# Modulation sums moved from VectorE to GpSimd, and the gather ticks and head choices of a fused transformer kernel placed anew

## The chip, the cores and the metric

The kernel runs on one core of a Trainium2 chip. The metric is the device time of one execution in microseconds, as the median of several runs. Before the change it is 1738.4 us (three runs, 1738.04 to 1740.64).

## What is computed

The input is one sequence of 256 rows by 1024 columns, in float32 throughout. A first block applies four mixers in turn (gated linear attention, a gated spatial unit, forgetting attention, gated linear attention again), each wrapped in an adaptive norm. A second block has a hybrid of convolution and dilated attention, and then a PEER layer: for every row, 8 heads choose 16 experts each out of 128 x 128, and every chosen expert is one row of a "down" table and one of an "up" table.

```python
def first_block(...):
    cond = silu(c)
    for i in range(DEPTH):                       # 4 mixers
        mod = (cond @ w_mod[i] + b_mod[i])[:, None, :]
        shift, scale, gate = split(mod, 3)
        h = rms_norm(x, norm_pre_g[i]) * (1.0 + scale) + shift
        ...                                      # mixer i on h, times gate, added to x
def peer_ffn(u, w_query, sub_keys, expert_down, expert_up):
    s = einsum('thcd,hckd->thck', q, sub_keys)
    top_s, top_i = top_k(s, 16)
    cand_s = top_s[:, :, 0, :, None] + top_s[:, :, 1, None, :]
    best_s, pos = top_k(cand_s.reshape(...), 16)
    idx, gates = take_along_axis(cand_i, pos), softmax(best_s)
    a = gelu(einsum('cd,ced->ce', u, expert_down[idx]))
    return einsum('ce,ced->cd', gates * a, expert_up[idx])
```

## The kernel before, in words

The 256 rows are two tiles of 128 partitions. One list, `ORDER` (made by `make_order`, line 357), holds every step of both tiles, and each engine walks the same list and emits its own share of each step; semaphores join the shares. A step `mm` (`project`, line 948) multiplies one block of 512 columns of a weight: 8 products of 128x128 by 128x512, whose weights SyncE loads into a ring of four halves of 1 MB. The first tile runs through all its mixers while blocks of the second tile are put into its gaps; behind that come the second tile's remaining blocks, and last its PEER layer alone.

**Modulation.** `cond @ w_mod` is a sum over eight slices k of the weight for each layer L and each third (shift, scale, gate): 96 pieces of 128x1024. A piece is fetched, and VectorE adds piece times cond's column into a sum (`add_piece`, line 1567). The first 16 come through `early` tiles, loaded by SyncE; six of these (`PE_PIECES`) are multiplied on TensorE instead (`piece_columns`, line 986). The other 80 are fetched by GpSimd's queue into a ring of four (`fetch`, line 849), each fetch behind a wait until VectorE has used the ring's place. The sums' biases are set by `start_sums` (lines 856 and 857), the gains behind the mixers are fetched by `fetch_post` (line 863). `mod_cols` (lines 1010 and 1831) turns shift and scale of a layer into columns, `mod_gate` (lines 1019 and 1839) spreads the gate over the partitions. `pieces_at` says behind which block the pieces are added: ahead of that block's own evacuation.

**Levels.** A gated linear attention mixer has seven levels (`level`, line 964). For each, VectorE makes exponents with two products of two operands in SBUF (lines 1581 and 1582), ScalarE takes their exponential (line 1365), VectorE multiplies twice more (lines 1590 and 1592), TensorE multiplies, and VectorE merges (line 1601).

**PEER.** `choose` (lines 1732 to 1781) finds one head's 16 experts in four parts. A `tick` is one chosen expert of all 128 rows: GpSimd issues its gathers (line 877), VectorE takes the product of the down row with the input (line 1798), ScalarE takes gelu of a group of these (line 1486, groups in `GROUPS`), VectorE forms the coefficients (line 1790), and `LEAD` ticks later the up row is added, on VectorE (line 1813) or on TensorE (lines 1493 and 1203). In the first tile, down and up rows are two gathers of 0.5 MB for each of 128 ticks; in the second, one gather of 1 MB. `Rows` hands out the ticks among the second tile's blocks by way gone (`WAY`), at most three behind a block (`spot`). Parts of the next head's choice hang on ticks 2, 4, 6 and 8 of a head.

## Time and profile before

| what | value |
|---|---|
| median of 3 runs | 1738.4 us |
| the profiled execution's own time | 1739.41 us |
| its span, first to last instruction | 1737.6 us |
| busy PE, DVE, ACT, POOL | 1393.7, 1047.5, 433.1, 490.7 us |
| mean granted TensorE clock | 0.909 |
| read from HBM | 589.55 MB, 340 GB/s over the span |

PE is TensorE, PEld its weight loads, DVE VectorE, ACT ScalarE, POOL GpSimd, SP SyncE; a q behind a name is its queue. In a row of the timeline the first number is the start and the second the length, both in us; what stands in brackets at its end is how long the engine was idle before it and what ended the idleness. The L numbers are lines of the kernel.

### The profile page before, as it was taken

How to read it: one execution, taken by the hardware profiler on the slowest of the kernel's cores; microseconds unless marked ns; L12 is line 12 of the kernel's file. 1: busy time of each engine (PE TensorE's matmuls, PEld its weight loads, DVE VectorE, ACT ScalarE, POOL GpSimd, SP SyncE). 2: the span in 40 equal slices, each digit the busy share in tenths (PEclk: the TensorE clock that was granted, in tenths of full speed). 3: DMA queues.
4: the chain of work that ended last, by engine and by line, in shares of the span. 5: the costliest groups of instructions: out<-in, count | busy, mean ns of one | idle time of the engine just before them, and what ended most of it. 6: DMA issues, size and time to landing. Idle time of an engine off the chain costs nothing. (4 is left out here: it accounts for less than half of the span.)

```text
span 1737.6 us, 13867 instructions
## 1 busy us (share of the span) xinstructions
PE 1393.7 (80%) x4158; PEld 717.6 (41%) x4158; DVE 1047.5 (60%) x2197; ACT 433.1 (25%) x974; POOL 490.7 (28%) x498
## 2 busy tenths in 40 slices
PE   6998988978999999999777777699787647666665
PEld 6454435444444455444354343455333312222222
DVE  3645554553233222313797998788866778877876
ACT  1221413423423421102133232132002221111111
POOL 2101210210000000000445546355344545444441
PEclk9998998989999999999897888798888878898898
DMA  9978884978556776887999989999999999999995
GB/s 386 377 256 303 312 340 171 347 282 295 213 207 219 277 265 242 290 293 265 402 361 357 413 339 403 412 400 413 410 414 414 348 412 422 421 422 421 422 421 248
DMA packets 108941, 591.53 MB, mean 340 GB/s; under 512 B 12450, under 2 KB 12706, under 8 KB 60612
## 3 DMA queue, kind: packets, MB, share of 16 engines
q0 software_dynamic: 67776, 312.56, 45.4%
q1 hardware_dynamic: 41092, 278.10, 42.2%
q8 instruction: 34, 0.56, 0.1%
q14 instruction: 39, 0.32, 0.0%
HBM read 589.55 MB, written 1.05 MB: 340 GB/s over the span
## 5 line engine op out<-in xcount | busy, mean ns | idle before, releaser
L948 PE MATMUL bank<-ring,hT 128*128 128x512 f32 x1888 | 866.6, 615 | 39.6 <-DVE room L1920 12.1
L948 PEld LDWEIGHTS bank<-ring,hT 128*128 128x128 f32 x1888 | 366.5, 198 | 482.2 <-issue 449.8
L877 POOL DMA_INDIRECT room<-in_peer_down,idx x92 | 102.5, 1114 | 525.1 <-DVE idx L1781 401.8
L1798 DVE CUSTOM_DVE_ANT_0 room<-room 128x1024 f32<-128x1024 f32 x180 | 218.6, 1221 | 50.6 <-DMA room<-in_pair,idx 38.4
L1203 PE MATMUL bank<-room 128*128 128x512 f32 x284 | 150.9, 676 | 96.5 <-ACT room L1493 94.2
L1813 DVE SCALAR_TENSOR_TENSOR x<-room,pcoef,x 128x1024 f32<-128x1024 f32 x121 | 155.7, 1287 | 28.0 <-DMA room<-in_peer_up,idx 27.5
L877 POOL DMA_INDIRECT room<-in_peer_up,idx x104 | 114.0, 1096 | 88.6 <-DVE pa L1798 42.3
L1203 PEld LDWEIGHTS bank<-room 128*128 128x128 f32 x284 | 57.5, 215 | 190.8 <-issue 97.2
L849 POOL DMA_DIRECT2D room<-in_w_mod x80 | 42.2, 528 | 326.3 <-DVE room L1567 206.5
L877 POOL DMA_INDIRECT room<-in_pair,idx x88 | 97.0, 1102 | 108.5 <-PE bank L1203 50.6
L927 PE MATMUL bank<-cst,room 128*128 128x128 f32 x424 | 64.7, 297 | 55.3 <-ACT room L1439 24.1
L1203 PE MATMUL bank<-ring,room 128*128 128x512 f32 x116 | 72.6, 774 | 38.0 <-ACT room L1493 38.0
L1567 DVE SCALAR_TENSOR_TENSOR room<-room,cst 128x1024 f32<-128x1024 f32 x58 | 74.4, 1282 | 36.0 <-DMA room<-in_w_mod 26.8
L927 PEld LDWEIGHTS bank<-cst,room 128*128 128x128 f32 x424 | 54.9, 153 | 82.4 <-ACT room L1439 26.8
L964 PE MATMUL bank<-room 128*128 128x128 f32 x256 | 43.9, 331 | 34.7 <-DVE room L1592 34.7
L1493 ACT ACTIVATE room<-cst,pcoef 128x128 f32<-128x128 f32 x102 | 36.8, 392 | 118.0 <-DVE pcoef L1790 110.8
L1439 ACT ACTIVATE room<-room,anm 128x128 f32<-128x128 f32 (+1 forms) x80 | 35.4, 443 | 116.3 <-DVE anm L2004 116.3
L877 POOL DMA_INDIRECT ring<-in_pair,idx x40 | 46.6, 1166 | 61.8 <-PE bank L1203 30.8
L1798 DVE CUSTOM_DVE_ANT_0 ring<-ring,room 128x1024 f32<-128x1024 f32 x40 | 48.8, 1226 | 23.1 <-DMA ring<-in_pair,idx 22.8
L1203 PEld LDWEIGHTS bank<-ring,room 128*128 128x128 f32 x116 | 26.7, 243 | 80.6 <-ACT room L1493 52.3
L964 PEld LDWEIGHTS bank<-room 128*128 128x128 f32 x256 | 40.0, 236 | 44.9 <-DVE room L1592 40.1
L1272 ACT ACTIVATE room<-bank 128x512 f32<-128x512 f32 x24 | 14.3, 596 | 147.0 <-PE bank L948 147.0
(304 smaller groups left out, 1527.4 us busy)
## 6 DMA issues: line engine op xcount, KB each, us to landing
ring<-in_wpk SPq DMA_DIRECT2D x248, 1024.0 KB, 7.0
room<-in_w_mod POOLq DMA_DIRECT2D x80, 512.0 KB, 8.2
room<-in_w_mod SPq DMA_DIRECT2D x8, 1024.0 KB, 15.8
room<-in_norm_post_g POOLq DMA_DIRECT2D x4, 512.0 KB, 5.0
rowb<-in_gate_bias SPq DMA_DIRECT2D x4, 512.0 KB, 9.0
room<-in_peer_up,idx POOLq DMA_INDIRECT x104, 12.5
room<-in_peer_down,idx POOLq DMA_INDIRECT x92, 12.4
room<-in_pair,idx POOLq DMA_INDIRECT x88, 14.3
```

What stands on the lines that cost most here:

```text
L849: pool.dma_start(mring[n % 4], w[:, k, third * D:(third + 1) * D]).then_inc(S(f"pool_in{n % 4}"), 16)
L877: return pool.indirect_dma_start(out=dst, out_offset=None, in_=A[table][0] if table != "pair" else A[table], in_offset=bass.IndirectOffset ...
L927: last = tr(cols4(b, i), src(i), ident)
L948: last = mm(bank[p][:, :], lhs, ring[:, h % 4, k * N:(k + 1) * N], start=(kk == 0), stop=(h == halves[-1] and k == 3))
L964: last = mm(cols4((b, c, a)[l % 3], h), k_[:, h * P:(h + 1) * P], q_[:, h * P:(h + 1) * P], start=True, stop=True)
L1203: last = mm(bank[WORK[tile][i]][:, :], diag[:, nth % 4, :], row[:, i * N:(i + 1) * N], start=(v == mine[0]), stop=(v == mine[-1]), skip_gr ...
L1272: af(dst, src, ACT.Copy).then_inc(done, 1)
L1439: last = af(s, s, ACT.Exp, bias=anm[:, t, n, h:h + 1], accum_out=al[:, t, n, h:h + 1])
L1493: af(diag[:, nth % 4, :], ident, ACT.Copy, scale=pcoef[:, v // TOPK % 4, v % TOPK:v % TOPK + 1]).then_inc(S("diag"), 1)
L1567: v.scalar_tensor_tensor(out=a, in0=piece, scalar=const("cond", k, 1), in1=a, op0=ALU.mult, op1=ALU.add).then_inc(S("summed"), 1)
L1798: v.tensor_tensor_reduce(out=row, in0=row, in1=u_(g // MINE), scale=1.0, scalar=0.0, op0=ALU.mult, op1=ALU.add, accum_out=pa[:, g // TOPK ...
L1813: v.scalar_tensor_tensor(out=x[:, tile, :], in0=row, scalar=pcoef[:, w, e:e + 1], in1=x[:, tile, :], op0=ALU.mult, op1=ALU.add) \
```

## The change

1. Pieces: the first 16 go to VectorE but for two on TensorE (six before). Of the 80 others, the 24 scales of layers 1 to 3 stay on VectorE and the 56 shifts and gates go to GpSimd, as two instructions each (a product, then a sum), through a ring of two places; the scales have the other two. `mod_cols` and `mod_gate` wait for GpSimd's count. VectorE's pieces now stand behind a block's own work. GpSimd's queue also carries the fetches of scales, some behind a wait for VectorE.
2. Ticks: also between the second tile's levels. The last eight picks are added two a tick, the last group of four is two of two, and four ticks at the end fall away. In `make_order` one block of the second tile stands earlier.
3. Choices: the first head's score is transposed and multiplied one block sooner, and its choice stands a block sooner. In the first tile a head's parts stand in the list by themselves, behind blocks with little VectorE work, or when they are due. Inside `choose`, casts fall away, and pairs of instructions over both halves become one.

```diff
-            "gap twice"]
+            "gap" if L == 2 else "gap twice"]
...
             b(3, [], [("unit", t, 1), ("forget_sum", t)]),
+            "gap",
...
-            b(0, name="query", pre=[("norm_in", t, 5)]),
-            b(1, [("score_T", t, 0)], name="query"),
-            b(2, [("score_S", t, 0), ("score_T", t, 1)], name="query"),
+            b(0, [] if t else [("score_T", t, 0)], name="query", pre=[("norm_in", t, 5)]),
+            b(1, [("score_T", t, 0)] if t else [("score_S", t, 0)], name="query"),
+            b(2, ([("score_S", t, 0)] if t else []) + [("score_T", t, 1)], name="query"),
...
-TICKS = PICKS + REST + LEAD[1]
-PE_PIECES = (5, 7, 9, 11, 13, 15)
+TICKS = PICKS + REST + 2
+FIRST = [(0, third, k) for third in range(2) for k in range(KC)]
+PE_PIECES = (5, 7)
+DVE_FIRST = len(FIRST) - len(PE_PIECES)
+DVE_PIECES = [(L, 1, k) for L in range(1, DEPTH) for k in range(KC)]
+POOL_PIECES = [(0, 2, k) for k in range(KC)] \
+    + [(L, third, k) for L in range(1, DEPTH) for third in (0, 2) for k in range(KC)]
...
 def added_at(v):
+    if v >= PICKS - 8:
+        return tick_of(PICKS - 2) + (v - PICKS + 8) // 2
     return tick_of(v) + LEAD[v // MINE]
...
+    def choose_light(self, most):
+        for _ in range(most):
+            if self.part < 4 * PH and self.at >= TOPK * (self.part // 4 - 1) - 6:
+                self.choose_next()
+    def choose_due(self):
+        while self.part < 4 * PH and self.at >= TOPK * (self.part // 4 - 1) + 3 + 2 * (self.part % 4):
+            self.choose_next()
...
+            elif s[0] == "level" and after[0] in ("level", "cross"):
+                spot(1)
...
+            def fetch(i):
+                if i >= len(POOL_PIECES):
+                    return
+                if i >= 2:
+                    pool.wait_ge(S("pool_summed"), i - 1)
+                pool.dma_start(mring[i % 2], piece_of(*POOL_PIECES[i])).then_inc(S(f"pool_in{i % 2}"), 16)
+            def fetch_scale(i):
+                pool.wait_ge(S("summed"), DVE_FIRST + max(i - 1, 0))
+                pool.dma_start(mring[2 + i % 2], piece_of(*DVE_PIECES[i])).then_inc(S(f"pool_in{2 + i % 2}"), 16)
+            def add_piece(i):
+                L, third, k = POOL_PIECES[i]
+                pool.wait_ge(S(f"sums_init{L % 2}"), sums_set(L))
+                pool.wait_ge(S(f"pool_in{i % 2}"), (i // 2 + 1) * 16)
+                link(nc.gpsimd.tensor_tensor(mring[i % 2], mring[i % 2], const("cond", k, 1).to_broadcast([P, D]), ALU.mult))
+                if i:
+                    pool.wait_ge(S("pool_summed"), i)
+                nc.gpsimd.tensor_tensor(sums[L % 2][third], sums[L % 2][third], mring[i % 2], ALU.add) \
+                    .then_inc(S("pool_summed"), 1)
+                fetch(i + 2)
...
+            pool.wait_ge(S("summed"), DVE_FIRST)
+            for i in range(2):
+                fetch(i)
+            for i in range(2):
+                fetch_scale(i)
+            for k in range(KC):
+                add_piece(k)
+                if k % 2:
+                    fetch_scale(2 + k // 2)
...
-                    pe.wait_ge(S("summed"), summed_before((L + 1) * 3 * KC))
+                    pe.wait_ge(S("pool_summed"), gates_of(L))
```

## Rows read from the trace of the kernel before

**Rows 1.** The page's slices: 40 equal parts of the span, and bytes moved.

```profile
PE   6998988978999999999777777699787647666665
...
GB/s 386 377 256 303 312 340 171 347 282 295 213 207 219 277 265 242 290 293 265 402 361 357 413 339 403 412 400 413 410 414 414 348 412 422 421 422 421 422 421 248
```

**Rows 2.** Stretches: length, busy PE, PEld, DVE, ACT, POOL, clock, DMA share, GB/s.

```profile
60.00:440.00 380.00, 328.99 (x1033) 175.02 (x1032) 193.18 (x334) 114.97 (x246) 48.30 (x87) 0.92 0.79 295
440.00:820.00 380.00, 363.07 (x1121) 182.55 (x1119) 105.64 (x286) 96.15 (x209) 0.00 (x0) 0.99 0.71 253
820.00:1380.00 560.00, 433.19 (x1420) 237.60 (x1420) 447.70 (x922) 140.29 (x309) 273.00 (x246) 0.87 0.98 391
```

**Rows 3.** The same view, stretches of 20 us.

```profile
900.00:920.00 20.00, 12.38 (x72) 11.17 (x70) 16.81 (x31) 9.18 (x17) 9.34 (x9) 0.68 0.80 278
1020.00:1040.00 20.00, 13.94 (x43) 8.79 (x44) 18.32 (x53) 9.77 (x23) 6.52 (x6) 0.83 0.75 269
1080.00:1100.00 20.00, 20.00 (x64) 10.02 (x63) 12.86 (x32) 3.46 (x5) 7.99 (x8) 1.00 1.02 415
```

**Rows 4.** Groups of instructions by line and form: busy us, mean ns, idle before.

```profile
L1567 DVE SCALAR_TENSOR_TENSOR room<-room,cst 128x1024 f32<-128x1024 f32 x58 | 74.4, 1282 | 36.0 <-DMA room<-in_w_mod 26.8 <-DMA room<-in_b_mod 8.0
L856 POOL MEMSET room<- 128x1024 f32 x8 | 7.8, 970 | 0.0
L1581 DVE TENSOR_TENSOR room<-room 128x256 f32<-128x256 f32 x28 | 11.7, 417 | 0.6 <-DVE room L1892 0.5
```

**Rows 5.** DMA issues, median us from issue to landing.

```profile
room<-in_w_mod POOLq DMA_DIRECT2D x80, 512.0 KB, 8.2
```

**Rows 6.** The timeline from 20 to 60 us: the first layer's columns.

```profile
25.49 13.65 PE L986 MATMUL bank<-cst,room 128*128 128x1 f32 x64
29.20 1.28 DVE L1567 SCALAR_TENSOR_TENSOR room<-room,cst 128x1024 f32<-128x1024 f32 x1 [1.27 <-DMA room<-in_w_mod]
46.00 0.17 DVE L1831 COPY modc<-bank 128x8 f32<-128x8 f32 x1 [15.52 <-PE bank L1010]
```

**Rows 7.** The timeline: a decay, and where the sums of layers 0 to 2 are due.

```profile
68.27 0.69 DVE L1615 SCALAR_TENSOR_TENSOR room<-bank,room 128x512 f32<-128x512 f32 x1 [2.44 <-ACT room L1354]
...
98.03 1.02 PE L1019 MATMUL bank<-room,ones 128*128 128x512 f32 x2
...
148.15 2.25 PE L1010 MATMUL bank<-ones,room 128*128 128x1 f32 x16
...
154.53 0.16 DVE L1831 COPY modc<-bank 128x8 f32<-128x8 f32 x1
...
287.54 3.63 PE L1010 MATMUL bank<-ones,room 128*128 128x1 f32 x32
```

**Rows 8.** TensorE's waits from 60 to 440 us: total, times, longest.

```profile
PE bank L964 <- DVE room L1592: 13.6, 7, 3.1
PE bank L948 <- DVE room L1920: 8.4, 3, 5.0
PE bank L1123 <- DVE room L1986: 7.1, 2, 4.4
PE bank L1019 <- DVE gateb L1839: 5.7, 1, 5.7
```

**Rows 9.** The timeline around the first head's choice.

```profile
811.26 0.49 DVE L1732 MAX8 pv<-room 128x8 f32<-128x128 f32 x2 [10.83 <-ACT room L1474]
821.25 1.00 POOL L877 DMA_INDIRECT room<-in_peer_down,idx  x1 [393.95 <-DVE idx L1781]
```

**Rows 10.** The timeline behind the second tile's last levels.

```profile
1023.05 1.24 POOL L877 DMA_INDIRECT room<-in_peer_up,idx  x1 [6.88 <-DVE pa L1798]
```

**Rows 11.** The timeline of the last 15 us.

```profile
1722.75 1.22 DVE L1798 CUSTOM_DVE_ANT_0 room<-room 128x1024 f32<-128x1024 f32 x1 [1.21 <-DMA room<-in_pair,idx]
1724.57 5.42 PE L1203 MATMUL bank<-room 128*128 128x512 f32 x12 [1.20 <-ACT room L1493]
1730.02 1.28 DVE L2086 TENSOR_TENSOR x<-x,bank 128x512 f32<-128x512 f32 x2 [0.72 <-PE bank L1203]
```

More of the change, by code:

```diff
@@ L272 @@
 DVE_NTH = {u: i for i, u in enumerate(ON_DVE)}
-ADDS = {added_at(v): [v] for v in range(PICKS)}
+ADDS = {k: [v for v in range(PICKS) if added_at(v) == k] for k in range(TICKS)}
 def adds_of(k):
-    return ADDS.get(k, [])
+    return ADDS[k]
 def sums_at(hh):
@@ L302, with light @@
        "z_T": 15, "att_in": 20, "b_T": 20, "merged_T": 40, "ffn_norm": 60, "score_T": 6, "score_S": 10}
+DVE_WORK = {"norm_in": 5, "low": 2, "decay": 25, "qk_T": 4, "level": 20, "cross": 25, "heads": 25, "post0": 7,
+            "post1": 50, "center": 30, "mix": 35, "unit": 40, "forget": 5, "forget_sum": 5, "quad_S": 27, "quad_V": 6,
+            "fox_gate": 14, "rotary": 18, "merge": 50, "z_T": 65, "b_T": 14, "ffn_norm": 20}
+def light(steps):
+    return sum(DVE_WORK.get(s[0], 0) for s in steps) <= 12
 def way_of(step):
@@ L320, in __init__ @@
         self.order, self.at, self.added = order, 0, 0
+        self.part = 4
     def add_next(self):
@@ L367, in make_order @@
             second.append(c)
-    done, pending, ahead, piece = 0, [], False, 2 * KC
+    done, pending, ahead, piece = 0, [], False, 0
     for c in first:
@@ L379, in make_order @@
             order.append(mm)
-        for _ in range(pieces_at(mm)):
-            if piece < len(PIECES):
-                order.append(("mod", piece))
-                piece += 1
         if mm and mm[2] in ("out0", "out1", "out2") and mm[3] == 1:
@@ L397, in make_order @@
                 order.append(("sines", 0))
+            for _ in range(PIECES_AT[name][n] if name in PIECES_AT else 0):
+                order.append(("mod", piece))
+                piece += 1
             order += pending
             pending = []
-            if name == "query" and n == 2:
-                order.append(("choose", 0))
-                rows.tick()
-            if name == "query" and n == 3:
-                rows.tick()
-                rows.tick()
+            if name == "query" and n == 1:
+                order += [("choose", 0, part) for part in range(4)]
+            if name == "query" and n >= 2:
+                for _ in range(n - 1):
+                    rows.tick()
     order += pending
@@ L432, in make_order @@
             if s == ("score_S", 1, 0):
-                order.append(("choose", PH))
+                order += [("choose", PH, part) for part in range(4)]
             if (s[0], after[0]) in (("quad_S", "quad_P"), ("cross", "heads")):
                 spot(2)
+            elif s[0] == "level" and after[0] in ("level", "cross"):
+                spot(1)
         if not (i + 1 < len(left) and left[i + 1][0]):
             spot(3)
+        if light(post):
+            rows.choose_light(2)
+    assert rows.part == 4 * PH
     while rows.at < TICKS:
@@ L992, in _ @@
             pe.wait_ge(S("cond"), 1)
-            for piece in PE_PIECES[:2]:
+            for piece in PE_PIECES:
                 piece_columns(piece, use("mod_cols", 0)[1])
@@ L2076, in _ @@
                 elif kind == "choose":
-                    for part in range(4):
-                        choose(t, part)
+                    choose(t, step[2])
                 elif kind == "tick":
```

146 lines of the change are left out of this document (74 added, 72 removed).

## The prediction

> **What bounds the kernel now.** I read the page's slices first. They show three stages: up to about 820 us TensorE is nearly always busy and the bytes stay far under their best rate; from there to 1380 us the rate is mostly over 400 GB/s and TensorE falls back; behind that it is 412 to 422 [rows 1]. The stretches put numbers to it: from 60 to 440 us TensorE is busy 329 of 380 us at a clock of 0.92, from 440 to 820 us 363 of 380 at 0.99, from 820 to 1380 us the DMA share is 0.98 [rows 2]. So up to 820 us the time is TensorE's with what it waits for, and behind that it is mostly the gathers'. An earlier start of the gathers moves the end with it, one for one, as long as nothing else becomes late.
>
> What is open before 440 us: 51 us of TensorE idleness, and 0.08 of the clock, 380 x 0.08 = 30 us. The waits name VectorE for most of it: 13.6 us at the levels, 8.4 behind the mixer's output, 7.1 before the scores, and one of 5.7 before a gate [rows 8]. What is open from 820 to 1380 us: at 391 GB/s on average against 415 in a full stretch, 560 x (1 - 391/415) = 32 us of transfer time [rows 2, 3]. Two of the holes are at 900 and 1020 us, of 20 x (1 - 278/415) = 6.6 and 20 x (1 - 269/415) = 7.0 us [rows 3].
>
> **The change, part by part.** The sum is made against the profiled execution's own 1739.4 us; the median of the runs shown is 1.0 lower.
>
> *The first columns.* TensorE spent 13.65 us on four pieces (64 records), to 39.1 us, and then made the columns, so that they were copied at 46.0; VectorE's last of ten pieces stood at 29.2 [rows 6]. With four more pieces of 1.28 [rows 4] among its 10, VectorE ends at about 33.4, and the columns, which took 46.0 - 39.1 = 6.9 us, need half of that behind it, as the shifts' half can go ahead: 37. That is 9 us sooner.
>
> *GpSimd's chain up to layer 1.* It takes what was won back. GpSimd has no arithmetic with operands in the trace of before; the nearest row is its memset of the same shape, 0.97 us, which only writes [rows 4]. From below I bound one instruction by that, from above by three times it, 2.9 (two reads and a write, one behind another). VectorE's 1.28 with two operands lies between. I take 2.4, toward the upper end, because nothing in the row says that reads are free. A piece is then 2 x 2.4 + 0.3 = 5.1 us. Each ring place goes round in 5.1 + 0.3 + 8.2 (issue to landing, [rows 5]) = 13.6 us, and there are two places: 6.8 us a piece. The first fetch waits for VectorE's 14 pieces (33.4) and lands near 44. The third piece stands behind a fetch of a scale that waits until VectorE has added its first one, behind the decay, whose first step stood at 68.3 [rows 7] and whose end now comes at some 62: 4.5 us more. The gates of layer 0, 8 pieces, then stand at about 99, where they were used at 98.0 and would now be wanted at 89 [rows 7]. Layer 1's shifts, 16 pieces: 44 + 7 x 13.6 + 6.3 + 5.1 + 4.5 = 155, and columns and copy 4.4 later, 159.5. Before, the copy was at 154.5 [rows 7]. So the term is **+5**, with the first columns' 9 us inside it. With 0.97 an instruction the chain is not late, and what is left is 9 sooner and 4 because VectorE no longer adds pieces right ahead of the copy: -13. With 2.9 it is +14. Layer 2's columns are due at 287.5 [rows 7] and need 32 pieces, which stand at 155 + 16 x 6.8 = 264; layer 3's are due later still for as many more. That cover is gone at over 8.2 us a piece. No gather waits in GpSimd's queue, for the first is at 821 [rows 9].
>
> The Trainium skill (GPSIMD Engine Reference, Elementwise) gives 4497 ns for such an addition of 2048 elements a partition, by which I would estimate 2.25 us for 1024; by it this term would be about +3. No run here shows it yet.
>
> *VectorE's relief, 60 to 440 us.* Of 90 pieces on VectorE 38 stay; 52 x 1.28 = 67 us go [rows 4]. Most of this lay beside TensorE. What TensorE waited for behind pieces I bound by the longest wait of each row, 3.1 + 5.0 + 4.4 + 5.7 = 18.2, and half of the 16.6 that these rows have besides: 26 us [rows 8]; the clock would give part of its 30 besides. I take half of the 26, **-12** rounded, and nothing for the clock, since other waits remain and will be late next (ScalarE's exponentials between a level's halves, the sums of squares). Ends: -40 (all 26 and half the clock) and 0.
>
> *The stage of gathers.* The first choice began at 811.3, when the score had come, and the first gather went out at 821.3 [rows 9]; one block sooner is about 8 us, in which VectorE still has to end the second tile's `unit` work. At 270 GB/s instead of 415 there, 8 x (1 - 270/415) = 2.8: **-3**. Ticks between levels and choices moved behind lighter blocks: GpSimd stood 6.9 us behind VectorE at the end of the levels [rows 10]; of the 14 us in the two holes I take half, **-7**. The casts saved in `choose` are under 1 us a head and lie beside transfers: 0. The ticks between levels make the second tile's levels longer, which costs nothing while transfers bind. Ends of this part: 0 and -25.
>
> *The end.* The last row's product starts at 1722.75; then come gelu, coefficients, three adds on TensorE (5.42 us from 1724.57), and the final sum at 1730.02 [rows 11]. Afterwards only picks 254 and 255 are left then, both on VectorE, two adds of 1.28 [rows 4] from about 1725.3: 1727.9. **-2**, ends -3 and 0.
>
> Sum: 1739.4 + 5 - 12 - 3 - 7 - 2 = 1720.4; less the 1.0 to the median, 1719.5. A measurement of this kernel tells about 0.2%, 3.5 us, from no change.
>
> **The rivals.**
>
> *A: GpSimd and VectorE stop each other (slower).* While a GpSimd instruction reads SBUF, VectorE's instructions with two operands in SBUF wait for its end. The place is the levels of layer 0 in both tiles, 14 levels with two pairs of such products each of 0.42 us [rows 4], with GpSimd busy 4.8 of 6.8 us. One wait of about 2.4 us a pair is 28 x 2.4 = 67 us on VectorE; half uncovered makes +34, and the other work up to 440 us +10. Instead of -19 the sum is +25: 1763. It decides from about 1.0 us a pair (28 x 1.0 / 2 = 14, and 4 for the rest), where the gain of 19 is gone. For it: TensorE already waited 13.6 us at the levels [rows 8], so there is no slack there. Against it: nothing in the trace of before shows VectorE slowed by GpSimd, though GpSimd reads no tensor there. Chance 0.23. This is a rule of the Trainium skill too (SBUF — State Buffer, Who interferes with whom): the second of the two to issue blocks fully until the first is done. No run here shows it yet.
>
> *B: the gain stays small (no change).* The chain is +5, VectorE's relief is a third (-4), because TensorE's own work is what is left, and of the gathers' part only -1: about 1739. For it: the clock below 1.0 stays whatever is idle. Chance 0.10.
>
> *C: only the gathers' side pays.* The relief is eaten by a later chain (+10, -12), and -8 comes behind 820 us, the end with it: 1728. Chance 0.15.
>
> *D: all open parts close.* -13 - 26 - 17 - 3 = -59: 1680. For it: the row of memset. Chance 0.07.
>
> *E: the ticks' new places do nothing*, since DMA is full anyway at 0.98 [rows 2]: 1727, taken together with C.
>
> **How the numbers follow.** The forecast has 0.45, for 1719.5. The range goes from 1700, half way to D, to 1758, most of the way to A; outside are D and the upper half of A. Faster: 0.45 + 0.15 + 0.07 = 0.67; no change 0.10; slower 0.23.
>
> **What would show it.** The `modc` copy of layer 1 at about 159 us; GpSimd's products and sums at 2 to 2.9 us; VectorE's lines 1581 to 1592 still at 0.42 us (rival A shows them longer, or TensorE's wait at the levels at 30 us and more); TensorE's stretch from 60 to 440 us some 12 us shorter to the same step; the first gather before 808; the holes behind the levels half filled; 5 us from the last landing to the final sum. Wrong would be: a gate's or column's wait of over 10 us for GpSimd, or a first gather later than 821.

## The result, and the profile after it

The changed kernel takes 1805.84 us (median of 4 runs, 1801.42 to 1810.19), the kernel before on the same chip 1739.52 (4 runs). The ratio is 1.0377, with a 95% interval from 1.0346 to 1.0409: slower by 66 us, where 19 us faster was forecast. The profiled execution has a span of 1799.6 us, against 1737.6 before; it is the shortest of the four runs, so the tables below account for 62 us and not for 66.

Three moments split both spans: the first gather, the first gather of a pair (where the second tile's own work is done), and the last row's product.

| | before | after | difference | forecast |
|---|---|---|---|---|
| to the first gather (stage A) | 821.3 | 860.0 | +38.7 | -10 |
| to the first gather of a pair (stage B) | 573.6 | 596.9 | +23.3 | -7 |
| to the last row's product (stage C) | 327.9 | 329.6 | +1.7 | 0 |
| to the end | 14.8 | 13.2 | -1.6 | -2 |

The forecast column puts each term into the stage in which it begins. Of a choice made 8 us sooner the prediction counted only 3 us for the end, so it had the first gather itself before 808, and gave some of that back in stage B.

The page of the kernel after: its slices, its groups of GpSimd's products and sums and of VectorE's scale pieces, and the landing of the pieces.

```profile
PE   5767876998798999999885856869987746666765
...
GB/s 387 307 227 287 279 316 230 213 331 247 238 205 184 262 254 262 257 318 249 389 411 314 359 373 326 366 355 413 415 415 415 371 387 420 421 420 421 421 420 264
...
L908 POOL TENSOR_TENSOR room<-room,cst 128x1024 f32<-128x1024 f32 x56 | 108.1, 1930 | 15.6 <-DMA room<-in_w_mod 12.3
...
L911 POOL TENSOR_TENSOR room<-room 128x1024 f32<-128x1024 f32 x24 | 60.4, 2515 | 1.9
...
L902 POOL DMA_DIRECT2D room<-in_w_mod x24 | 12.8, 533 | 107.1 <-DVE room L1652 107.1
L1652 DVE SCALAR_TENSOR_TENSOR room<-room,cst 128x1024 f32<-128x1024 f32 x24 | 46.6, 1940 | 15.6 <-DMA room<-in_w_mod 15.2
...
room<-in_w_mod POOLq DMA_DIRECT2D x80, 512.0 KB, 5.3
```

GpSimd's instructions came as estimated (1.93 and 2.5 us for the 2.4 assumed), and the pieces land sooner than in [rows 5] (5.3 us, not 8.2). So the lengths of GpSimd's own instructions are not what was mis-sized. But the same VectorE sum that took 1.28 us in [rows 4] takes 1.94 here, and L902 shows 107.1 us in which GpSimd stood, with its own pieces behind it, at fetches that wait for VectorE.

Stretches, with the columns of [rows 2]:

```profile
60.00:440.00 380.00, 299.80 (x916) 160.73 (x915) 220.56 (x266) 98.22 (x212) 253.47 (x175) 0.87 0.73 265
...
860.00:1457.00 597.00, 454.69 (x1466) 247.95 (x1464) 452.41 (x881) 146.37 (x322) 296.68 (x257) 0.87 0.96 378
```

In the same 380 us TensorE does 916 matmuls where it did 1033, at a clock of 0.87 for 0.92. VectorE, which should have been relieved, is busy 221 us where it was 193. TensorE's waits in that stretch, beside [rows 8] (L1044 and L1100 are L964 and L1019 of before):

```profile
PE bank L1044 <- DVE room L1677: 39.7, 9, 6.1
PE bank L1100 <- DVE gateb L1915: 11.4, 1, 11.4
PE bank L1028 <- DVE room L1996: 9.8, 3, 6.8
```

The timeline, 76.66 to 89.07 us, in the first tile's levels of layer 0:

```profile
77.33 0.41 DVE L1667 TENSOR_TENSOR room<-room 128x256 f32<-128x256 f32 x1
77.77 0.43 DVE L1675 TENSOR_TENSOR room<-room 128x256 f32<-128x256 f32 x1
78.10 2.17 POOL L908 TENSOR_TENSOR room<-room,cst 128x1024 f32<-128x1024 f32 x1 [0.25 <-DMA room<-in_w_mod]
78.11 0.42 DVE L1677 TENSOR_TENSOR room<-room 128x256 f32<-128x256 f32 x1
78.56 2.00 DVE L1666 TENSOR_TENSOR room<-room 128x256 f32<-128x256 f32 x1
...
80.36 2.40 POOL L911 TENSOR_TENSOR room<-room 128x1024 f32<-128x1024 f32 x1
80.48 2.55 DVE L1667 TENSOR_TENSOR room<-room 128x256 f32<-128x256 f32 x1
82.96 0.41 DVE L1675 TENSOR_TENSOR room<-room 128x256 f32<-128x256 f32 x1
...
83.30 2.55 DVE L1677 TENSOR_TENSOR room<-room 128x256 f32<-128x256 f32 x1
...
85.63 2.43 POOL L911 TENSOR_TENSOR room<-room 128x1024 f32<-128x1024 f32 x1
85.76 0.72 DVE L1686 COPY_PREDICATED room<-gmask,bank 128x512 f32<-128x512 int32 x1
85.90 1.78 PEld L1044 LDWEIGHTS bank<-room 128*128 128x128 f32 x8 [5.69 <-DVE room L1677]
```

A level product takes 0.41 us while GpSimd computes nothing (77.33, 82.96), and 2.00 or 2.55 us when a product or sum of GpSimd is under way: it ends when GpSimd's ends (78.56 + 2.00 = 80.56; 80.48 + 2.55 = 83.03). The one at 78.11 starts together with GpSimd's product and keeps its 0.42 us; there the product is the longer one, 2.17 us for a mean of 1.93. TensorE then waits 5.7 us where [rows 8] had 3.1 at most. This is rival A as it was written, and the rule of the Trainium skill (SBUF — State Buffer, Who interferes with whom), that the second to issue blocks fully; the trace agrees.

### The profile page after: what moved, and what is told of

It is laid out like the page before. It is cut to its first block and busy times, and to the rows that moved or that the text cites. A ratio compares the mean times of both kernels' runs of the same rounds, so it can differ in the third digit from the quotient of the medians.

```text
span 1799.6 us, 13758 instructions
## 1 busy us (share of the span) xinstructions
PE 1397.9 (78%) x4094; PEld 713.6 (40%) x4094; DVE 1079.9 (60%) x2050; ACT 436.0 (24%) x977; POOL 759.7 (42%) x610
## 5 line engine op out<-in xcount | busy, mean ns | idle before, releaser
L1874 DVE CUSTOM_DVE_ANT_0 room<-room 128x1024 f32<-128x1024 f32 x174 | 211.4, 1221 | 62.8 <-DMA room<-in_pair,idx 41.1
L1284 PE MATMUL bank<-room 128*128 128x512 f32 x284 | 160.1, 713 | 95.5 <-ACT room L1575 93.3
L1889 DVE SCALAR_TENSOR_TENSOR x<-room,pcoef,x 128x1024 f32<-128x1024 f32 x127 | 163.4, 1286 | 36.1 <-DMA room<-in_peer_up,idx 35.4
L957 POOL DMA_INDIRECT room<-in_peer_up,idx x110 | 129.0, 1172 | 84.6 <-DVE pa L1874 34.1
L1284 PEld LDWEIGHTS bank<-room 128*128 128x128 f32 x284 | 61.1, 227 | 193.0 <-issue 103.5
L1007 PE MATMUL bank<-cst,room 128*128 128x128 f32 x424 | 66.1, 300 | 68.2 <-DVE room L1618 27.3
L908 POOL TENSOR_TENSOR room<-room,cst 128x1024 f32<-128x1024 f32 x56 | 108.1, 1930 | 15.6 <-DMA room<-in_w_mod 12.3
L1044 PE MATMUL bank<-room 128*128 128x128 f32 x256 | 49.0, 355 | 75.1 <-DVE room L1677 75.1
L1284 PE MATMUL bank<-ring,room 128*128 128x512 f32 x116 | 65.5, 705 | 39.2 <-ACT room L1575 39.2
L1044 PEld LDWEIGHTS bank<-room 128*128 128x128 f32 x256 | 44.0, 256 | 86.3 <-DVE room L1677 81.6
L911 POOL TENSOR_TENSOR room<-room 128x1024 f32<-128x1024 f32 x24 | 60.4, 2515 | 1.9
L902 POOL DMA_DIRECT2D room<-in_w_mod x24 | 12.8, 533 | 107.1 <-DVE room L1652 107.1
L1652 DVE SCALAR_TENSOR_TENSOR room<-room,cst 128x1024 f32<-128x1024 f32 x24 | 46.6, 1940 | 15.6 <-DMA room<-in_w_mod 15.2
(305 smaller groups left out, 1720.4 us busy)
```

The lines of the kernel that those rows point to most:

```text
L908: link(nc.gpsimd.tensor_tensor(mring[i % 2], mring[i % 2], const("cond", k, 1).to_broadcast([P, D]), ALU.mult))
L911: nc.gpsimd.tensor_tensor(sums[L % 2][third], sums[L % 2][third], mring[i % 2], ALU.add) \
L957: return pool.indirect_dma_start(out=dst, out_offset=None, in_=A[table][0] if table != "pair" else A[table], in_offset=bass.IndirectOffset ...
L1007: last = tr(cols4(b, i), src(i), ident)
L1044: last = mm(cols4((b, c, a)[l % 3], h), k_[:, h * P:(h + 1) * P], q_[:, h * P:(h + 1) * P], start=True, stop=True)
L1284: last = mm(bank[WORK[tile][i]][:, :], diag[:, nth % 4, :], row[:, i * N:(i + 1) * N], start=(v == mine[0]), stop=(v == mine[-1]), skip_gr ...
```

## Experiments

Ratios are to runs of the kernel before on the same chip. "A" is the first gather, "B" the stage behind it, both from one profiled execution. One kernel was profiled twice and gave 808.6 and 812.2 for A, and the kernels whose stage B is as before or nearly so give 572.7 to 578.0 for B (in one case 582.2); smaller differences than these say nothing by themselves. "The lock" is short for what the last timeline shows: an instruction of VectorE and one of GpSimd of which one waits for the other's end.

### The parts of the change

**Modulation alone** (pieces to GpSimd, VectorE's scale pieces, the first columns; nothing of ticks, choices, gaps or end):

```
(in words) POOL_PIECES, DVE_PIECES, add_scale, fetch_scale and PIECES_AT as in the change;
           make_order's ticks, choices and gaps, and the end, as in before
```

> The kernel before with the modulation part of the change alone (shifts and gates on GpSimd, pieces' new places, two pieces on TensorE). Theory 1 (GpSimd and VectorE stop each other, and that is most of the loss): first gather some 35 to 50 us later than before's 821 us, in all 1775 to 1790 us; the level products (128x256, two operands in SBUF) near 0.9 us again instead of 0.42. Theory 2 (the loss comes from the new places of ticks and choices): within 5 us of before. The changed kernel's stage of gathers was 23 us longer too; if that is the ticks' doing, this run shows none of it: from first gather to first gather of the second tile 574 us as before.

1775.71 us, 1.0151 (1.0111 to 1.0190); A 852.7, B 577.5. By the ratio this part costs 26 us (19 to 33), by the first gather 31; B is within what unchanged kernels show.

**Everything but the modulation:**

```
(in words) all hunks of the change but those of sums, pieces and PIECES_AT;
           pieces_at, add_piece and PE_PIECES as in before
```

> The changed kernel with the modulation as before: only ticks, choices, the tail and the blocks' order are changed. Theory 1 alone: faster than before by some 5 to 12 us. If the new places of ticks and choices are a loss by themselves, as the 23 us longer stage of gathers in the changed kernel suggests: 1750 to 1765 us, with the first gather some 8 us sooner than before's 821 us and the stage of gathers near 597 instead of 574 us.

1759.94 us, 1.0086 (1.0056 to 1.0116); A 817.1, B 596.4. Slower too: 4 us sooner in A, which is within what one kernel shows, and 23 lost in B. So there are two losses, and each shows without the other: the two spans are 38.1 and 20.1 us longer than before's, 58 together, where the whole change has 62. In A they do not simply add up: the modulation part is worth 31 us alone (852.7 for 821.3) and 43 beside the rest (860.0 for 817.1). Why is open.

**The first columns alone:**

```
-PE_PIECES = (5, 7, 9, 11, 13, 15)
+PE_PIECES = (5, 7)
```

> The kernel before with pieces 9, 11, 13 and 15 on VectorE instead of TensorE, nothing else. The first layer's columns are copied near 37 instead of 46 us. If nothing later holds, 1730 us (9 less); if VectorE's pieces from 48 us on hold the end of the first mixer anyway, 1736 to 1739 us.

1741.85 us, 0.9981 (0.9960 to 1.0001), not told from no change. The columns are copied at 36.92 instead of 46.0 (37 forecast), yet A is 821.5 (821.3 before). What is won is lost again later: layer 1's columns come at 151.0 for 154.5, layer 3's at 445.6 in both. One row also made it look larger than it is: in the traces of kernels with the old first columns the copy stands anywhere from 42.2 to 46.2, so the columns come 5 to 9 us sooner.

### The lock

**Memsets for GpSimd's product and sum** in the kernel after (the kernel leaves shifts and gates out of the result):

```
-nc.gpsimd.tensor_tensor(mring[i % 2], mring[i % 2], cond, ALU.mult)
+2 x nc.gpsimd.memset(mring[i % 2], 0.0)
-nc.gpsimd.tensor_tensor(sums, sums, mring[i % 2], ALU.add)
+3 x nc.gpsimd.memset(sums, 0.0)
```

> The changed kernel, with GpSimd's product replaced by two memsets and its sum by three of the same tile (4.9 us a piece against 4.4): the same waits and places, the modulation's shifts and gates left out. Theory 1a (VectorE waits because GpSimd reads SBUF): level products back at 0.42 us and TensorE's wait at the levels near 14 us; first gather 825 us or sooner, in all 1755 to 1770 us. Theory 1b (the loss is the length of GpSimd's chain, not the lock): first gather still at 855 to 870 us, in all 1800 us or more.

1784.69 us, 1.0217 (1.0178 to 1.0257); A 842.5, B 596.0. Groups of VectorE with their forms up to the first gather, this kernel, and below it the kernel after:

```profile
L1654 DVE SCALAR_TENSOR_TENSOR room<-room,cst 128x1024 f32<-128x1024 f32 x24 | 30.8, 1282 | 55.7 <-DMA room<-in_w_mod 55.4
...
L1668 DVE TENSOR_TENSOR room<-room 128x256 f32<-128x256 f32 x21 | 8.8, 418 | 0.6 <-DVE room L1970 0.5
```

```profile
L1666 DVE TENSOR_TENSOR room<-room 128x256 f32<-128x256 f32 x21 | 24.2, 1154 | 0.6 <-DVE room L1968 0.5
...
L1686 DVE COPY_PREDICATED room<-gmask,bank 128x512 f32<-128x512 int32 x24 | 17.3, 722 | 6.8 <-PE bank L1044 6.4
```

Without GpSimd's reads every VectorE form with two operands in SBUF is back at its old duration; the one that copies out of a PSUM bank (L1686, 0.72 us) was never longer. So the lock is shown, and it is worth 17 us of A (860.0 to 842.5); if anything that is too little, for memsets hold up other forms of VectorE (last section). But theory 1a had 825 or sooner, and 842.5 is still 25 us behind the 817.1 of the kernel with the old modulation: a second cause.

**The lock with nothing moved**, and its comparison. The kernel before, with work for GpSimd on the free ring place ahead of each fetch:

```
 def fetch(n):
     pool.wait_ge(S("summed"), ...)
+    2 x nc.gpsimd.tensor_tensor(mring[n % 4], mring[n % 4], cond, ALU.mult)   (first run)
+    4 x nc.gpsimd.memset(mring[n % 4], 0.0)                                  (second run)
```

> The kernel before, nothing moved, with two products of GpSimd (128 partitions by 1024, both operands in SBUF) on a free place of the ring ahead of each of its 80 fetches of a piece; VectorE still adds all 90 pieces. If GpSimd's reads stop VectorE (theory A), VectorE's sums of 1.28 us and its level products of 0.42 us come out at 1.6 to 2.5 us wherever GpSimd is at it, and the kernel takes 15 to 40 us more than the same kernel with memsets in their place. If the lock needs something else of the change, both kernels take the same time to 4 us.

> The kernel before with four memsets of GpSimd (about 0.97 us each, nothing read) ahead of each fetch of a piece, as the comparison for the run with two products: the fetches are held up about as long. Theory A: VectorE's sums stay at 1.28 us and its level products at 0.42 us; the time is that of the kernel before or up to 8 us more, for the later fetches alone.

1874.55 us, 1.0772 (1.0733 to 1.0811), against 1813.74 us, 1.0406 (1.0365 to 1.0446). One row of each, groups of VectorE with their forms from 60 to 500 us, first the products, then the memsets:

```profile
L1569 DVE SCALAR_TENSOR_TENSOR room<-room,cst 128x1024 f32<-128x1024 f32 x41 | 103.7, 2529 | 26.6 <-DMA room<-in_w_mod 25.8
```

```profile
L1569 DVE SCALAR_TENSOR_TENSOR room<-room,cst 128x1024 f32<-128x1024 f32 x44 | 56.4, 1283 | 68.4 <-DMA room<-in_w_mod 67.9
```

1874.55 - 1813.74 = 61 us is the lock, above the 15 to 40 expected: 160 products of 2.1 us, and VectorE's sum of 1.28 takes 2.53. The comparison missed its own bound of 8 us by far (it lost 72): the pieces' fetches come late by four memsets each, and VectorE waits 105 us for them (67.9, 27.3 and 10.1 in its three groups). The ring of pieces was no place with slack.

### The rest of stage A

In the run with memsets VectorE stood 35 us at its first scale piece of layer 2; in the modulation part alone 17.6 us, and there GpSimd stood 21.6 us at the fetch of the next one. The timelines of the two kernels, first VectorE with memsets, then VectorE and GpSimd of the modulation alone:

```profile
210.17 1.29 DVE L1654 SCALAR_TENSOR_TENSOR room<-room,cst 128x1024 f32<-128x1024 f32 x1 [34.96 <-DMA room<-in_w_mod]
```

```profile
205.82 1.28 DVE L1620 SCALAR_TENSOR_TENSOR room<-room,cst 128x1024 f32<-128x1024 f32 x1 [17.56 <-DMA room<-in_w_mod]
...
233.20 2.65 DVE L1620 SCALAR_TENSOR_TENSOR room<-room,cst 128x1024 f32<-128x1024 f32 x2
234.78 0.54 POOL L870 DMA_DIRECT2D room<-in_w_mod  x1 [21.55 <-DVE room L1620]
```

Both engines work in order, and each has work behind a wait for the other: VectorE the second tile's levels behind a piece that GpSimd has not fetched, GpSimd its own pieces behind a fetch whose place VectorE has not read.

**VectorE's pieces of layer 2 later**, in the kernel with memsets and in the modulation part alone:

```
-"in1": (1, 2, 2, 2, 1, 0)
+"in1": (0, 0, 2, 2, 2, 2)
```

> The kernel after with GpSimd's product and sum replaced by memsets of the same cells (shifts and gates are left out of the result), and VectorE's eight scale pieces of layer 2 put one to two blocks later in its order. Theory I (VectorE works in order, and a scale piece for which GpSimd has not even issued the fetch holds the second tile's levels behind it, 35 us in the run with memsets): the wait of 35 us is gone or under 10, and the first gather comes at 815 to 825 us instead of 842.5, the kernel at 1755 to 1767 instead of 1784.7. Theory F (GpSimd's fetches are simply too late for layer 2, wherever VectorE asks for them): the columns of layer 2 are as late as in the run with memsets (323 us) and the first gather stays past 835 us.

> The modulation part alone (1775.7 us), with VectorE's eight scale pieces of layer 2 one to two blocks later in its order. Theory I (VectorE's scale pieces and GpSimd's fetches of them stand in two queues that wait for each other): TensorE's wait of 17.0 us at the second tile's levels of layer 1 goes, the first gather comes 10 to 15 us sooner than 852.7, and the time is 1761 to 1767 us. Theory G (the lock and GpSimd's pace are all there is): the first gather stays within 4 us of 852.7 and the time over 1771 us.

With memsets: 1771.44 us, 1.0157 (1.0128 to 1.0185), A 828.6, between the two theories; 14 of the 25 us come back. With the lock: 1777.79 us, 1.0219 (1.0181 to 1.0256), A 851.8: nothing. Theory I failed there. The wait only moved: TensorE now stands 22.5 us at the second tile's levels, at 273.8, because VectorE's pieces come one for each piece of GpSimd, 6.6 us apart (fetched at 238.5, 245.2, 251.9, 258.5).

**The fetches by SP:**

```
(in words)
-GpSimd: fetch_scale(i) between its own pieces
+SP, ahead of the weights two blocks on: wait for the sum of piece i - 2, then fetch piece i
```

> The modulation part alone (1775.7 us), with the 24 fetches of VectorE's scale pieces issued by SP, two blocks ahead of their use, instead of by GpSimd between its own pieces. Theory K (VectorE's scale pieces come at GpSimd's pace, one for each product and sum of GpSimd, 6.6 us apart, and GpSimd itself stands up to 21.6 and 31.6 us behind VectorE at such fetches; both waits come from the shared queue): these waits go, TensorE's waits of 17.0 and 11.1 us at 213 and 266 us are under 8 together, the first gather comes at 835 to 845 us instead of 852.7, the time is 1758 to 1768. Theory G (the lock alone is what costs): the first gather stays over 849 us.

> The same fetches by SP in the kernel in which GpSimd's product and sum are memsets (1784.7 us; shifts and gates are left out of the result), with the ticks between levels and the choices' places of the change. With neither the lock nor the shared queue left, theory K gives the first gather at 812 to 822 us, as with the modulation part of before (817.1), or sooner by what the prediction hoped for (12 us); the stage of gathers stays at 596 us and the time comes to 1752 to 1764. If the first gather stays past 830 us, GpSimd's pace of 5.8 us a piece is a cause of its own.

With the lock: 1784.39 us, 1.0260 (1.0212 to 1.0308), A 852.3. The two engines' waits for each other over these fetches are gone, and the time is not better. Theory K failed in its number. SP's waits up to 500 us and TensorE's from 60 to 852 us show what is late next:

```profile
SPq L790 <- DVE room L1627: 134.7, 20, 18.0
```

```profile
PE bank L1019 <- DVE room L1652: 43.2, 14, 6.6
PE bank L1003 <- issue: 13.0, 3, 9.2
```

SP, which also issues the weights' loads, now stands 134.7 us at scale pieces, and TensorE has waits of 13.0 us in all for which the profile names no releaser ("issue"); that these are late weights is likely and not shown. The levels' waits stay at 43.2 us, 14 of them; before, the same group had 18.7 us (11 times) on the whole way. With memsets and SP: 1772.60 us, 1.0162 (1.0113 to 1.0211), A 839.9, not the 812 to 822 of theory K. There VectorE waits 34.0 us, once, at 200 us, for the start of layer 2's accumulators, which GpSimd reaches only behind its 24 pieces of layers 0 and 1. So the second cause is a group: whatever of layer 2 VectorE wants stands in GpSimd's queue behind layer 1's gates. In the best of these runs (828.6 for 817.1) three long waits of TensorE are left: a gate of layer 0 that GpSimd has not summed, the next gate, and a level behind two scale pieces for which VectorE itself waits (5.2 and 1.6 us).

```profile
101.29 2.04 PE L1102 MATMUL bank<-room,ones 128*128 128x512 f32 x2 [12.04 <-POOL room L914]
...
237.64 2.07 PE L1102 MATMUL bank<-skT,ones 128*128 128x512 f32 x2 [10.46 <-DVE gateb L1917]
...
260.89 1.44 PE L1046 MATMUL bank<-room 128*128 128x128 f32 x5 [13.23 <-DVE room L1679]
```

Stretches from 60 us to the first gather, this run and under it the one with the old modulation:

```profile
60.00:828.60 768.60, 679.35 (x2108) 349.76 (x2107) 241.78 (x559) 211.16 (x452) 307.03 (x360) 0.94 0.74 267
```

```profile
60.00:817.10 757.10, 684.34 (x2125) 351.72 (x2124) 296.58 (x613) 212.22 (x454) 47.42 (x85) 0.96 0.75 271
```

TensorE is idle 89.2 us here and 72.8 there. The three waits are 35.7 us of the 89.2; in the other trace the same places have about 7 (5.1, 1.7 and none). So all other waits fell from about 66 to about 54 us, by 12: this is an estimate from two traces, but it closes, for 29 - 12 - 5 (TensorE's busy time, 679.35 for 684.34) is 12 and A differs by 11.5. So a relief is there, and the waits for GpSimd's order are more than twice as long.

### Stage B

**Without ticks between levels; with the choices back on the ticks; with both taken back** (all three without the modulation part):

```
-            elif s[0] == "level" and after[0] in ("level", "cross"):
-                spot(1)
```

```
-        self.choose_due()
...
-        if light(post):
-            rows.choose_light(2)
...
-                if PH < hh + 1 < T * PH and e in (2, 4, 6, 8):
+                if hh + 1 < T * PH and hh + 1 != PH and e in (2, 4, 6, 8):
```

> The change without its modulation part (1759.9 us), and also without the ticks between the second tile's levels. Theory L (those ticks put a row's product or add of VectorE, 1.2 to 1.3 us each, into a chain of levels on which TensorE waits, and so the stage from the first gather to the first gather of a pair is 23 us longer): the stage comes back to 573 to 577 us and the time to 1738 to 1742 us. Theory H (the head choices in their new places are what costs): the stage stays at 593 to 597 us and the time at 1756 to 1760 us.

> The change without its modulation part (1759.9 us), with the second tile's head choices on the rows' ticks 2, 4, 6 and 8 as in the kernel before, the ticks between levels kept. Theory L (ticks between levels cost): the stage of gathers stays at 590 to 597 us, the time at 1753 to 1760 us. Theory H (the choices' new places cost): the stage is back at 573 to 580 us, the time at 1736 to 1745 us.

> The kernel before with what is left of the change when the modulation part, the ticks between levels and the choices' new places are all taken back: the first head's choice a block sooner, one gap fewer behind a layer's output and one more ahead of the fourth block, merged choice instructions, the last picks on VectorE. If L and H together are the whole of the longer stage: 573 us for it, and 1735 to 1738 us for the kernel, some 4 us from the sooner first gather and 1.5 us from the end below the kernel before. If the gaps or the merged instructions are the cause, it stays at 1750 us or more.

| levels' ticks | choices' places | us | ratio | B |
|---|---|---|---|---|
| new | new | 1759.94 | 1.0086 | 596.4 |
| old | new | 1766.58 | 1.0130 (1.0098 to 1.0163) | 605.6 |
| new | old | 1752.66 | 1.0050 (1.0030 to 1.0071) | 590.8 |
| old | old | 1737.81 | 0.9972 (0.9949 to 0.9994) | 576.7 |

Neither theory was right alone: each part costs by itself, 14 us of B (ticks) and 29 us (choices), and together 20. TensorE's timeline at the norm of layer 3 and at the next norm, with the choices' new places, and under it the first of them without:

```profile
944.10 1.97 PE L957 MATMUL bank<-cst,room 128*128 128x128 f32 x8 [13.53 <-DVE room L1566]
...
1075.99 1.97 PE L957 MATMUL bank<-cst,room 128*128 128x128 f32 x8 [15.78 <-DVE room L1566]
```

```profile
940.06 1.97 PE L953 MATMUL bank<-cst,room 128*128 128x128 f32 x8 [7.51 <-DVE room L1562]
```

VectorE's timeline of the kernel with the new places says why: between the two halves of a layer's output stand two parts of the third head's choice, from 932.29 to 938.3, and only then the output's second half, its norm and the levels.

```profile
932.29 0.47 DVE L1762 MAX8 pv<-room 128x8 f32<-128x128 f32 x2
...
938.13 0.17 DVE L1788 TENSOR_SCALAR pab<-ppos 128x16 uint32<-128x16 uint32 x1
938.33 0.69 DVE L1941 TENSOR_TENSOR room<-bank,gateb 128x512 f32<-128x512 f32 x1
```

13.53 - 7.51 = 6.0 us, the two parts' own length. A step with little VectorE work of its own is light because its chain runs elsewhere for a moment; VectorE is wanted again at once.

**Those places no longer light:**

```
-"low": 2, ... "qk_T": 4, ... "post0": 7
+"low": 50, ... "qk_T": 50, ... "post0": 50
```

> The change without its modulation part and without ticks between levels (1766.6 us), with the places behind the first half of a layer's output, behind the decay's low part and behind the transposed queries no longer counted as light, so that no two parts of a head's choice stand there. Theory P (a choice of 3 us a part in those places stands ahead of the steps for which TensorE waits: 13.5 instead of 7.5 us at the norm, 19.4 instead of 13.1 at the first level, 15.8 instead of 9.1 at the second norm): these three waits are back at 7.5, 13 to 16 and 9 us, the stage of gathers takes 576 to 590 us instead of 605.6, and the kernel 1738 to 1751 us. Theory Q (a head's choice in parts costs wherever it stands off the ticks, because the indices come too late or too early): the stage stays over 598 us.

1746.32 us, 1.0019 (0.9998 to 1.0041), 20 of the 29 us back; B is 590.5, which is 15 of its 29. The three waits are 7.52, 13.25 and 9.78 us. Theory P holds for these three places. The other 14 us of B were not taken apart.

The ticks between levels cost by the same means. From the second tile's first level to the norm behind that layer TensorE's timelines give 66.6 us without them (991.1 to 1057.7) and 83.2 with them (996.0 to 1079.2): 16.6 us longer, for five more ticks (19 adds for 14), each a row's product and an add of 2.5 us together, in a chain. VectorE is busy 72.8 us of the longer stretch and 61.5 of the shorter.

What this looks like in the transfers is in the stretches from 5 us behind the first gather to the end of stage B. They move 393 GB/s with neither part, 383 with the levels' ticks, 374 with the choices' places, 379 with both. Against the 415 of a full stretch [rows 3] that is 30, 45, 59 and 51 us of transfer time not used. This is the same difference told in bytes and no second proof: all four move the same amount in stage B (rate times length agree to 0.3%), so a longer stage must show a lower rate. What tells the chain from the transfers are the runs, in which only the places of VectorE's work differ. Row places come free only with VectorE's products and adds, and these stand in the same queue as the chain.

### What is worth keeping

**The same without the changed gaps:**

```
-            "gap" if L == 2 else "gap twice"]
+            "gap twice"]
-            "gap",                               (ahead of the fourth block)
```

> The kernel before with the sooner first choice, the merged choice instructions and the last picks on VectorE, but with the gaps of the kernel before (the run with the changed gaps: 1737.8 us). If the gaps do nothing: 1736 to 1740 us and the first gather at 816 to 819 us. If they are what brings the first gather 4 us ahead: 820 to 822 us and 1740 to 1743.

**The end and the merged instructions alone; the gaps alone; and the best once more:**

```
tail_only: before + merged choice instructions + last picks on VectorE (choice 0 behind query block 2)
gap_only:  before + "gap" if L == 2 else "gap twice", and a "gap" ahead of the fourth block
best:      before + merged instructions + last picks + choice 0 behind query block 1
```

> The kernel before with the merged choice instructions and the last picks on VectorE alone; the first head's choice where it was before. If the sooner choice is what brings the run without gap changes to 1729.3 us: 1736 to 1740 us, the first gather at 819 to 823 us, 13 us from the last product to the end. If the merged instructions bring it: 1728 to 1733.

> The kernel before with the changed gaps alone, that is with the second tile's first block of layer 1 some four blocks sooner among the first tile's. If the gaps cost what lies between the two runs with and without them (1737.8 and 1729.3 us): 1744 to 1750 us, the first gather at 825 to 831 us. If that difference was another's: 1738 to 1743.

> The kernel before with the sooner first choice, the merged choice instructions and the last picks on VectorE, a second time, beside kernels that have one of these parts: 1727 to 1733 us, 0.990 to 0.995 of the kernel before. The prediction's terms for these parts were 3 and 2 us, which would give 1735; the first gather at 807 to 811 us says that the sooner choice is worth its whole block.

| | us | ratio | A |
|---|---|---|---|
| best, the first time | 1729.29 | 0.9922 (0.9898 to 0.9946) | 808.6 |
| end and merged only | 1737.59 | 0.9963 (0.9937 to 0.9990) | 819.2 |
| gaps only | 1747.57 | 1.0026 (1.0006 to 1.0045) | 817.1 |
| best, once more | 1730.97 | 0.9919 (0.9888 to 0.9950) | 812.2 |

The first and the last row are one and the same kernel. At 1729.3 it lay below what either theory of the run without gaps had. It beats both kernels: 14 us below the kernel before, some 75 below the changed one. The sooner first choice brings about 7 of them (1737.59 - 1730.97; the two intervals just overlap). In the best kernel's timelines, beside [rows 9]:

```profile
802.91 0.49 DVE L1757 MAX8 pv<-room 128x8 f32<-128x128 f32 x2 [3.53 <-ACT room L1499]
```

```profile
812.20 1.00 POOL L902 DMA_INDIRECT room<-in_peer_down,idx  x1 [389.36 <-DVE idx L1796]
```

The choice starts 8.4 us sooner, VectorE's wait ahead of it is 3.5 us instead of 10.8, and stage B is no longer for it (574.6). The gaps cost 0.26%, or about 5 us, by themselves (0.06 to 0.45%); the two medians with and without them beside the other parts lie 8 apart (1737.81 and 1729.29). Their place in the trace was not pinned down: the expectation had the first gather at 825 to 831 us, it came at 817.1, and the single profile of that run (1739.6 us) does not show the loss. So that the gaps cost is measured, and how is open.

## Why the prediction was wrong

**Wrong in direction, in two places.** The modulation part was forecast at +5 - 12 = -7 and measured at +43 beside the rest of the change (860.0 for 817.1): the sum let VectorE run free beside GpSimd, where the lock of rival A held it (17 us), and it priced the queue that fetches for both engines at 4.5 us once, where that queue and its order cost much of the other 25. The new places of ticks and choices were forecast at -7 and measured at +20 to +23: the step that called a longer chain of levels free while transfers bind was wrong. In the order of the prediction:

*The first columns.* Right: copied at 37.28 for 37. The working was looser than that: VectorE's last piece started at 29.2 and ended at 30.5, and four more behind it would end at 35.6; they ended at 33.6, since the waits for the early pieces went too. What is won does not reach the first gather (821.5 with this part alone).

*GpSimd's chain up to layer 1, +5.* The chain itself kept its times: layer 0's eight gates stand at 99.2 (99 forecast), layer 1's shifts, the 16th sum, at 145.0 (155). Yet layer 1's copy came at 178.51 for 159. What was late there is VectorE: its four scans ahead of the copy take 7.44 us beside GpSimd and 1.37 before, and TensorE's own order was 22 us behind by then (its products for the columns start at 169.0 for 146.8). With memsets the copy came at 155.8. After, and below it before:

```profile
171.04 7.44 DVE L1704 TENSOR_TENSOR_SCAN room<-ones,room 128x128 f32<-128x128 f32 x4
178.51 0.17 DVE L1907 COPY modc<-bank 128x8 f32<-128x8 f32 x1
...
179.26 1.76 DVE L1596 SCALAR_TENSOR_TENSOR var<-sum,bias 128x1 f32<-128x1 f32 x1
```

```profile
142.20 1.37 DVE L1619 TENSOR_TENSOR_SCAN room<-ones,room 128x128 f32<-128x128 f32 x4
```

From layer 2 on, the step that failed is the one that priced the shared queue of fetches at 4.5 us once: GpSimd stood 107 us in all at VectorE's pieces, and VectorE up to 17.6 us (modulation alone) or 35 us (with memsets) at a piece not yet fetched. The cover was put as a pace ("gone at over 8.2 us a piece"). It was gone by order: what VectorE wanted of layer 2 stood behind layer 1's gates.

*VectorE's relief, -12.* It did not come in the changed kernel, where VectorE is busy 339 us from 60 us to the first gather and 299 before: the lock gave back more than the 52 pieces took away. That it is nothing in itself is not shown. With memsets, and VectorE's pieces later, VectorE is busy 242 us, and TensorE's other waits are about 12 us shorter, the size that was forecast; there it is the waits for GpSimd's order (12.0, 10.5 and 13.2 us) that keep the first gather at 828.6, behind the 817.1 with all pieces on VectorE. So the term was added beside a chain at +5 that was not at +5. No run has the relief without GpSimd's late sums and fetches.

*Rival A, chance 0.23, 1763 us.* Its mechanism is what happened; it was given too little chance for want of a row, though the prediction itself named the rule of the Trainium skill (SBUF — State Buffer, Who interferes with whom), and the trace agrees with it: 0.42 us became 2.00 to 2.55. Its size in stage A is 17 us where 34 + 10 was put; that its 1763 lies nearer to 1805.8 than the forecast does is in part luck, for it held neither the shared queue nor stage B. It reaches further than the levels it was priced at: VectorE is busy 339 us from 60 us to the first gather, 244 with memsets, 95 us more. Neither later pieces nor fetches by SP answered it: A stayed at 851.8 and 852.3 for 852.7.

*The stage of gathers.* The sooner choice was worth a whole block, 7 us and not 3: stage B kept its length (574.6), so the second tile's chain moved with the start, and not only bytes. The -7 for ticks between levels and lighter places was the worst step: +20 to +23. "The ticks between levels make the second tile's levels longer, which costs nothing while transfers bind" is wrong. Stage B ends when the second tile's chain ends, and the DMA share of 0.98 in [rows 2] does not say the contrary: in [rows 3]'s two holes VectorE was busy 16.8 and 18.3 of 20 us, and the runs with a longer chain have a longer stage B (590.8, 605.6 and 596.4 us for 576.7). No rival had this loss: E had the places doing nothing, and D and the forecast had them gain.

*The end, -2.* Right: -1.6. Over all traces the old end takes 14.8 to 17.2 us and the new one 13.2 to 14.7.

So the sum that happened, in profiled spans, is 1737.6 + 38.7 + 23.3 + 1.7 - 1.6 = 1799.7. (The forecast's own last step, 1720.4 less 1.0, is 1719.4.) Of the 38.7, the lock is 17.4 (860.0 - 842.5), the rest of the modulation part 25.4 (842.5 - 817.1), and what comes with everything else -4.2 (817.1 - 821.3). This last one is hardly more than the 3.6 us by which two profiles of one kernel differ, and it holds the sooner choice, which brings 7 us, and the gaps, which take as much or more away again beside it (817.5 with both, 808.6 and 812.2 without the gaps).

## What to carry to other kernels

Before work goes to a second engine, look at what it shares with the first: here the way to operands in SBUF (a product of 0.42 us waited for the end of a sum of 2.4) and the queue that fetches for both. Price a wait by what stands behind it in order on both engines, not by the pace of either. A place with little work on an engine is not a free place: ask how soon the chain needs that engine again. And a stage whose transfers are 98% busy can still be set by the chain that frees their buffers.

## What the runs showed of the hardware

- VectorE's instructions with two operands in SBUF and GpSimd's products and sums wait for each other's end: 0.42 us becomes 2.55 beside a sum of 2.4. The smallest is held as well: in the kernel after, an operation of one column with two operands took 1.76 us (L1596, at 179.26) where it takes 0.15 to 0.16 otherwise. GpSimd's own instructions are longer at times too: most products take 1.9 us and five 2.1 to 2.3, most sums 2.3 to 2.4 and nine 3.2 or more.
- Memsets of GpSimd block none of the two-operand forms: 0.42 and 1.28 us in both runs with memsets.
- Memsets are not free of effect: VectorE's norm with one operand (128x512) takes 0.48 us on the mean before, 0.73 in the kernel with memsets for GpSimd's work, and 0.85 in the one with four memsets a fetch (from 60 to 500 us). Some forms with one operand of 16 columns take 0.97 us in the kernel with memsets for GpSimd's work, and 0.17 otherwise. The norm's form with two operands did not change (0.75).
- Forms that read a PSUM bank (copies out of it under a mask, 0.72 us; products with a bank, 0.69) are unchanged beside GpSimd.
- GpSimd's product of 1024 columns with one column spread over them takes 1.93 us on the mean, its sum of two full tensors 2.5; the estimate of 2.25 from the Trainium skill (GPSIMD Engine Reference, Elementwise) lies between.
